# A decoder layer of three head groups on one core: both keys groups computed as a pair with tokens stationary, then turned

## The reference

```python
h = rmsnorm(x, norm_g)
q_a, k_a, v_a, g_a, u_p, g_p, q_m, g_m = split(h @ w_in)   # 1024 x4, 512 x4 columns
mem_k, mem_v = split(rmsnorm(mem, mem_norm_g) @ w_mem_kv)   # 256 memory tokens, 512 + 512
y_a = causal_attention(q_a, k_a, v_a) * silu(g_a)           # 8 heads x 128, one block of 256 keys
y_p = window_means(u_p) @ w_pool * pool_scale * silu(g_p)
y_m = memory_attention(q_m, mem_k, mem_v) * silu(g_m)       # 4 heads x 128
out = rmsnorm(x + concat(y_a, y_p, y_m) @ w_out, final_norm_g)
```

## Time and profile before

| | us |
|---|---|
| median of three executions | 429.81 (429.79 to 430.31) |
| the profiled execution | 429.81 |
| its span | 428.0 |
| TensorE busy | 419.6 |
| VectorE busy | 304.0 |
| ScalarE busy | 241.5 |
| GpSimd busy | 39.6 |

### The profile page before, as it was taken

The page is one execution under the profiler, slowest core; times in us unless marked ns, Lnnn a source line. Parts: engine busy times, 40 slices in busy tenths (PEclk is TensorE's granted clock), DMA queues, the critical chain, the costliest instruction groups (busy, mean ns, idle before and its releaser), DMA issues.

```text
span 428.0 us, 5922 instructions
## 1 busy us (share of the span) xinstructions
PE 419.6 (98%) x2244; PEld 361.7 (85%) x2244; DVE 304.0 (71%) x331; ACT 241.5 (56%) x325; POOL 39.6 (9%) x64
## 2 busy tenths in 40 slices
PE   9999999999999999999999999999999999999993
PEld 8888888888888888888888888888899888888882
DVE  5876865266786699857466878877667488897853
ACT  6764784284263766464465446555565566765611
POOL 1000000000050000000000232302000211000160
PEclk9999999999999999999999999999999999999998
DMA  8999969989979628645337256565646999468023
GB/s 277 415 413 420 410 201 371 131 270 361 157 185 270 249 100 306 222 159 196 100 106 239 98 172 213 158 196 155 239 149 208 252 415 279 174 241 297 3 84 112
DMA packets 28251, 96.34 MB, mean 225 GB/s; under 512 B 3776, under 2 KB 4288, under 8 KB 27328
## 3 DMA queue, kind: packets, MB, share of 16 engines
q1 hardware_dynamic: 24624, 83.26, 57.7%
q0 software_dynamic: 1152, 4.19, 5.4%
q10 hardware_dynamic: 2448, 8.52, 5.1%
HBM read 93.87 MB, written 2.10 MB: 224 GB/s over the span
## 4 chain that ended last, share of the span: by engine, by line
PE 95%; issue 2%; DVE 1%; POOL 0%; POOLq 0%; DVEq 0%
PE ps L622 36%; PE ps L625 18%; PE ps L640 4%; PE ps L638 4%; PE ps L639 4%; PE ps L681 3%; PE ps L679 3%; PE ps L680 3%; PE ps L662 3%; PE ps L664 3%; PE ps L663 3%; PE ps L603 3%; PE ps L610 1%; PE ps L759 1%; PE ps L714 1%
## 5 line engine op out<-in xcount | busy, mean ns | idle before, releaser
L1097 DVE TENSOR_TENSOR w_lo<-w_raw,w_hi 128x1024 fp32r<-128x1024 f32 x133 | 165.7, 1262 | 74.0 <-ACT w_hi L862 73.6
L622 PE MATMUL ps<-xT,w_hi 128*128 128x512 f32 x640 | 202.0, 397 | 0.0
L862 ACT ACTIVATE w_hi<-w_raw 128x1024 fp32r<-128x1024 f32 x133 | 138.0, 1055 | 84.0 <-PE ps L625 60.7
L625 PEld LDWEIGHTS ps<-xT,w_lo 128*128 128x128 f32 x640 | 120.2, 188 | 28.4
L625 PE MATMUL ps<-xT,w_lo 128*128 128x256 f32 x640 | 125.8, 278 | 0.0
L622 PEld LDWEIGHTS ps<-xT,w_hi 128*128 128x128 f32 x640 | 97.8, 189 | 0.4
L974 ACT ACTIVATE part_b<-ps 128x1024 f32<-128x1024 f32 x11 | 11.3, 1025 | 17.7 <-PE ps L625 17.7
L638 PE MATMUL ps<-w_hi,yT 128*128 128x512 f32 x46 | 17.9, 389 | 0.0
L639 PE MATMUL ps<-w_lo,yT 128*128 128x512 f32 x46 | 17.9, 389 | 0.0
L640 PE MATMUL ps<-w_hi,yT 128*128 128x512 f32 x46 | 17.9, 389 | 0.0
L862 ACT ACTIVATE w_hi<-x_f 128x1024 fp32r<-128x1024 f32 x8 | 8.5, 1060 | 10.5 <-PE ps L681 5.1
(11 more groups left out here) (208 smaller groups left out, 620.5 us busy)
## 6 DMA issues: line engine op xcount, KB each, us to landing
w_raw<-in_w_in SPq DMA_DIRECT2D x94, 512.0 KB, 4.5
w_raw<-in_w_out SPq DMA_DIRECT2D x30, 512.0 KB, 5.2
w_raw<-in_w_mem_kv SPq DMA_DIRECT2D x13, 512.0 KB, 12.4
x_t_raw<-in_x_t SPq DMA_DIRECT2D x8, 256.0 KB, 13.0
rows<-in_x ACTq DMA_DIRECT2D x2, 1024.0 KB, 9.9
rows<-in_mem ACTq DMA_DIRECT2D x2, 1024.0 KB, 12.6
x_f<-in_w_in SPq DMA_DIRECT2D x4, 512.0 KB, 6.7
x_f<-in_w_in POOLq DMA_DIRECT2D x4, 512.0 KB, 11.5
```

Of the source, the lines that this page charges most:

```text
L622: pe.matmul(ps[:, bank0(g) + f, :], hi[:, t, f * P:(f + 1) * P], moving[:, kt], start=(kt == 0), stop=(kt == KT - 1), skip_group_check=True)
L625: m = pe.matmul(ps[:, bank0(g) + f, 0:S], lo[:, t, f * P:(f + 1) * P], moving[:, kt, 0], start=False, stop=(kt == KT - 1), skip_group_chec ...
L862: act.activation(halves_of(n)[0], whole_of(n), ACT.Copy).then_inc(hi_done, 1)
L1097: dve.tensor_tensor(lo, whole_of(n), hi.bitcast(F32), ALU.subtract).then_inc(lo_done, 1)
```

## The change

K0 and K1 become a pair too, units 32 to 53, and the values' pair follows at units 54 to 75. Both use the same sums of activations. The keys then end with tokens on the rows, in `k_tok`; sixteen transposes on TensorE after the tenth unit of the values' pair (`turn_keys`) turn them, and ACT copies them to `kT`. In return for the features-on-rows form, 1/rms is multiplied in when the keys leave the accumulators, and no row of 1/rms is needed for them.

With it move: the sums of activations from K0's units to Q0's (`X_SUM_STEPS`); the loads and adding transfers of the pair's sums from K0's stretch to between Q1's loads; new ones for the values' pair into `v_f4` and again `x_f567`; the memory's rows into buffers of their own, at the same unit 20; the reading back of `rstd_rows` from unit 24 to 28 and from 36 to 46 (the writes stay at 22 and 34); and POOL's scaling of the memory's keys behind all eight adding transfers. The line numbers of the changed kernel are other ones.

```diff
-PAIRS = ((V0, V1), (OUT1, OUT2))
...
+PAIRS = ((K0, K1), (V0, V1), (OUT1, OUT2))
+KP, VP, OP = range(len(PAIRS))
+PAIR_UNITS = tuple(pair_units(*p) for p in PAIRS)
+PAIR_LOADS = tuple(pair_loads(*p) for p in PAIRS)
...
+K_PAIR = K0 * PPG
+V_PAIR = K_PAIR + IN_PAIR
+V_END = V_PAIR + IN_PAIR
...
-X_SUM_STEPS = {K0 * PPG + 2: 0, K0 * PPG + 3: 1, K0 * PPG + 4: 2, K0 * PPG + 5: 3}
...
+X_SUM_STEPS = {Q0 * PPG + 2: 0, Q0 * PPG + 3: 1, Q0 * PPG + 4: 2, Q0 * PPG + 5: 3}
...
-X_MEAN, MEM_MEAN = 20, 32
-SPREAD_WRITE, SPREAD_READ = {22: 0, 34: 1}, {24: 0, 36: 1}
+X_MEAN, MEM_MEAN = 20, 31
+SPREAD_WRITE, SPREAD_READ = {22: 0, 34: 1}, {28: 0, 46: 1}
+K_TWO, K_TURNED, K_COPIED = V_PAIR + 6, V_PAIR + 9, V_PAIR + 11
...
-            with sp.Fori(0, K1 - Q0) as g:
-                for a in range(PPG):
-                    sp.wait_ge(lo_done, g * PPG + (PPG + a + 1))
-                    sp.dma_start(w_raw[:, a], in_dram[bass.ds(g, 1), a].rearrange("g p t c -> p (g t) c")
-                                 ).then_inc(landed[a], 16)
+                load(p, dram, g - OUT0 if q == OP else IN_COLUMN[g], a)
+
+            def first_of_sums(q, f, dst, dram, column):
+
+                for i in range(BLOCKS):
+                    sp.dma_start(dst[:, i], dram[column, 2 * i]).then_inc((f4_landed, f5_landed)[f][q][i], 16)
+
+            for a in range(PPG):
+                sp.wait_ge(lo_done, MV * PPG + a + 1)
+                load(Q0 * PPG + a, in_dram, IN_COLUMN[Q0], a)
             for a in range(PPG):
                 if a == 1:
                     sp.wait_ge(x_lo, PPG)
-                    for i in range(BLOCKS):
-                        sp.dma_start(x_f4[:, i], in_dram[V1 - Q0, 2 * i]).then_inc(f4_landed[0][i], 16)
+                    first_of_sums(KP, 0, x_f4, in_dram, IN_COLUMN[K1])
                 if a == 5:
-                    for i in range(BLOCKS):
-                        sp.dma_start(x_f567[:, i, 0], in_dram[V0 - Q0, 2 * i]).then_inc(f5_landed[0][i], 16)
-                sp.wait_ge(lo_done, K0 * PPG + a + 1)
-                load(K1 * PPG + a, in_dram, K1 - Q0, a)
-            for r, (g, a) in enumerate(V_LOADS):
+                    first_of_sums(KP, 1, x_f567[:, :, 0], in_dram, IN_COLUMN[K0])
+                sp.wait_ge(lo_done, Q0 * PPG + a + 1)
+                load(Q1 * PPG + a, in_dram, IN_COLUMN[Q1], a)
+            for r, (g, a) in enumerate(PAIR_LOADS[KP]):
...
-                pair_load(0, V_PAIR + r, in_dram, Q0, g, a)
+                    slot_free(KP, *PAIR_LOADS[KP][r - RAW])
+                if r == RAW:
+                    sp.wait_ge(squared, 8)
+                    first_of_sums(VP, 0, v_f4, in_dram, IN_COLUMN[V1])
+                pair_load(KP, FIRST_PIECE[KP] + r, in_dram, g, a)
+            for r, (g, a) in enumerate(PAIR_LOADS[VP]):
+                if r < RAW:
...
+                if r == 4:
+                    sp.wait_ge(lo_done, unit_in(KP, M4, BLOCKS - 1) + 1)
+                    first_of_sums(VP, 1, x_f567[:, :, 0], in_dram, IN_COLUMN[V0])
+                pair_load(VP, FIRST_PIECE[VP] + r, in_dram, g, a)
...
-            for i in range(2):
+            def rstd_of(i):
+
...
+            rstd_of(0)
+            add_f4(KP, x_f4, in_dram, IN_COLUMN[K0])
+            add_f5(KP, x_f567, in_dram, IN_COLUMN[K0])
+            rstd_of(1)
+            add_f4(VP, v_f4, in_dram, IN_COLUMN[V0])
+            add_f5(VP, x_f567, in_dram, IN_COLUMN[V0])
+            pool.wait_ge(evacuated, V1 + 1)
             pool.wait_ge(rstd_spread[1], 16)
             pool.tensor_tensor(mkT[:, :, :], mkT[:, :, :], mem_rstd[:, :, :].to_broadcast([P, NF, M]),
                                ALU.mult).then_inc(mk_scaled, 1)
...
+            def turn_keys():
+
+                pe.wait_ge(evacuated, K1 + 1)
+                for f in range(2 * NF):
+                    for h in range(TH):
+                        c = (f % 2) * S + h * P
+                        m = pe.transpose(ps[:, bank0(K0) + f // 2, c:c + P], k_tok[:, h, f * HD:(f + 1) * HD], ident[:, :])
+                m.then_inc(k_turned, 1)
...
+                if n == K_PAIR:
+                    pe.wait_ge(evacuated, Q0 + 1)
                 if n == V_PAIR:
-                    pe.wait_ge(evacuated, K0 + 1)
-                if V_PAIR <= n < V_END:
+                    pe.wait_ge(evacuated, Q1 + 1)
+                if in_pair(n):
                     unit_of_pair(n)
+                    if n == K_TURNED:
+                        turn_keys()
                     continue
...
+                if a == 0 and g == U:
+                    pe.wait_ge(kT_ready, 2)
...
+            def spread(n):
+
+                if n in SPREAD_WRITE:
+                    i = SPREAD_WRITE[n]
+                    act.wait_ge(rstd_ready, i + 1)
+                    for h in range(TH):
+                        act.dma_start(rstd_rows[i, h].rearrange("(p a) -> p a", a=1), rstd_in[:, i, h:h + 1]
+                                      ).then_inc(rstd_written[i], 16)
+                if n in SPREAD_READ:
+                    i = SPREAD_READ[n]
+                    act.wait_ge(rstd_written[i], 16 * TH)
+                    act.dma_start((x_rstd, mem_rstd)[i][:, 0, :], rstd_rows[i].rearrange("(a h) p -> a (h p)", a=1)
+                                  .partition_broadcast(P)).then_inc(rstd_spread[i], 16)
+
...
+                    if n == K_COPIED:
+                        act.wait_ge(k_turned, 1)
+                        act.wait_ge(f67_done, sums_done(VP, F6, BLOCKS - 1))
+                        for j in range(2):
+                            act.activation(kT[:, NF * j:NF * (j + 1), :].rearrange("p (b f) s -> p b (f s)", b=2),
+                                           ps[:, bank0(K0) + 2 * j:bank0(K0) + 2 * j + 2, :], ACT.Copy).then_inc(kT_ready, 1)
...
-                        evacuate(K1)
+                    if n == K_PAIR + 12:
+                        evacuate(Q1)
+                    if n == K_PAIR + 16:
+                        dve.wait_ge(rstd_ready, 1)
+                        first_of_pair(*of_keys)
+                    if n == K_TWO:
+                        second_of_pair(*of_keys)
                     if n == V_PAIR + 16:
-                        values_one()
```

More of the change, by code:

```diff
@@ L152, in build @@
         qT = sb("qT", [P, 2 * NF, S], F32, early)
+        stage = ExitStack()
+        mem_rows_a = sb("mem_rows_a", [P, D], F32, stage)
+        stage.close()
+        stage = ExitStack()
+        v_f4 = sb("v_f4", [P, BLOCKS, TPP, COLS], F32, stage)
+        stage.close()
         kT = sb("kT", [P, 2 * NF, S], F32, early)
@@ L377, in whole_of @@
             g, i = unit(n)
-            sums4, sums567 = ((x_f4, x_f567), (f4, f567))[pair_of(n)]
+            sums4, sums567 = ((x_f4, x_f567), (v_f4, x_f567), (f4, f567))[pair_of(n)]
             return sums4[:, i] if g == N5 else sums567[:, i, {M4: 0, M1: F6, N7: F7}[g]]
@@ L539, in _ @@
                                ALU.mult).then_inc(mk_scaled, 1)
-            for k in range(BLOCKS):
-                pool.wait_ge(f4_landed[0][k], 16)
-                pool.dma_start(x_f4[:, k], in_dram[V0 - Q0, 2 * k], accum_op=ALU.add).then_inc(f4_summed[0][k], 16)
-            for k in range(BLOCKS):
-                pool.wait_ge(f5_landed[0][k], 16)
-                pool.dma_start(x_f567[:, k, 0], in_dram[V0 - Q0, 2 * k + 1], accum_op=ALU.add).then_inc(f5_summed[0][k], 16)
             def block_sums(i):
@@ L670, in pair_piece @@
                 g, a = unit(n)
-                rows = (xT, yT)[pair_of(n)]
+                rows = yT if pair_of(n) == OP else xT
                 for t in range(TPP):
@@ L1101, in weight_sum @@
                 p = piece_of(unit_in(q, M6 if f == F6 else M3, i))
-                sums4, sums567 = ((x_f4, x_f567), (f4, f567))[q]
+                sums4, sums567 = ((x_f4, x_f567), (v_f4, x_f567), (f4, f567))[q]
                 dve.wait_ge(landed[p % RAW], 16 * (p // RAW + 1))
@@ L1136, in split_sums, with first_of_pair @@
                                   ALU.subtract).then_inc(s_split, 1)
[L1138 removed]
+            def first_of_pair(qp, dst, scales):
                 first = slice(0, COLS)
[L1141 to L1143 removed]
+                one, two = PAIRS[qp]
+                dve.wait_ge(snapped, snaps_done(qp, SNAPS[M4, 1]))
+                settle(dve.tensor_tensor(dst[:, 1, first], dst[:, 1, first],
```

191 lines of the change are left out of this document (95 added, 96 removed).

## The result

The changed kernel takes 442.4 us (median of five executions, 441.6 to 443.6), the kernel before 429.8 on the same chip: a ratio of 1.0293, 95% interval 1.0274 to 1.0312. Slower, as forecast, but 5.4 us more than the 437 predicted and 1.4 above the range. The profiled execution took 443.6 us, with a span of 441.8.

The account below looks back on a forecast made before the run. TensorE's work was taken to bound the kernel. 428.0 - 1.7 (TensorE's work) + 8.3 (late Q1 piece) + 1.0 (ACT's lost lead) = 435.6 us of span, plus 1.8 outside it: 437 us, range 428 to 441.

Parts of the forecast that it names:

- What bounds the kernel, and the wait that takes over: Whole kernel: TensorE's work bounds it, 419.6 of 428.0 us; then TensorE idles before Q1's last units for late pieces, 8.3 us.
- TensorE's sum: Keys' pair and transposes on TensorE: -3.8 us for pairing, +1.75 for transposes, +0.3 for a wait, in all -1.7 us.
- the wait: Before the transposes in the values' pair: TensorE waits for DVE to take K1's half out, 0.3 us, bounds 0 and 1.4.
- ACT's chain: Start of the keys' pair: ACT, without lead, still has two squares, a copy and high parts to do; 1 us more.
- the first rival: Q1's loads: adds at the plain price, write delays nobody, last piece lands at 86.5, no wait; 428.1 us, chance 0.18.
- The bill of the moved transfers: DMA queue before Q1's last piece: transfers sum to 35.1 us, landing at 97.5, 8.3 us after the needed 89.2.
- The write of `rstd_rows`: Among Q1's loads, issued at 69.55: DMA engines then move next to nothing; lost time 3.5 to 5.3 us, taken as 4.5.
- Two adding transfers for `x_f567`: Around Q1's last two pieces: these start as those move and share the DMA engines with them; up to 5.8 us.
- The second write at 0 to 4.5: Keys' pair, unit 34: the write finds an emptier queue and costs 0, at most another 4.5 us.
- half of it: Q1's loads: write's stop or second adds fall outside, landing at 91.8 to 93; 428.5 to 433 us, chance 0.22.
- the third, the fallen clock: Behind a wait for a late piece: four units at half clock, up to 4 x 2.8 us more; 441 to 446, chance 0.05.
- The rule weighed against it: Q1's loads: 2.0 us per transfer plus bytes at 436 GB/s, adds unpriced; queue ends at 84 us, no wait, 428.1 us.

Follow-up runs that it names:

- everything out of the way: The change with three Q1 pieces before the wait for `xT`, `x_f567` loads after Q1's last, memory's rows at unit 16, writes at 64 and 76; 428.3 us.
- the write moved: The changed kernel with x's 1/rms written after unit 44 instead of 22 and read back after 50 instead of 28; 432.5 us.
- `x_f567` last: The changed kernel with the two loads for `x_f567` issued behind Q1's last piece instead of ahead of its last three; 447.2 us.
- plain adds: The changed kernel with the keys' pair's four adding transfers as plain loads, additions left out, write left in place; 436.1 us.

## Why the prediction missed, and what of it was right

**What bounds the kernel, and the wait that takes over: right.** Eleven loads from 59.5 on, TensorE idle in front of Q1's last units behind a load of `w_raw`, no wait above 0.2 us in the keys' pair: as written. The low GB/s came later and lasted longer, from 81 to 90 instead of 77 to 83.

**TensorE's sum: right.** From the start of the keys' pair to U are 84.8 us (193.17 - 108.41). The prediction's terms give twice 40.81, 1.75 for the transposes, 0.3 for the wait and 1.0 for ACT's chain: 84.7. The transposes took 1.97 and did not wait, and the first four half units took 6.42 (108.41 to 114.83) instead of 5.44, which is the 1.0 for ACT's chain. Without waits the change was worth what the sum on TensorE said: 428.3 was measured with everything out of the way, against 428.1 worked out for the first rival.

**The bill of the moved transfers: the step that failed.** Q1's last piece landed at 103.06 instead of 97.5. That is 5.6 us, and the time is off by 5.4. The path was right, its size was not: two terms of the bill were mis-sized, in opposite directions:
- "The write of `rstd_rows`": 4.5 us, with 3.5 to 5.3 as bounds. It cost 13.2. The bounds were lost time read where one piece at a time or a few stood beside the write. Beside a queue of plain loads the same write cost 7.6, beside adds 13.2, where its stop came twice. So bounds from the emptier stretch did not hold in the crowded one, and the sum had no term for what write and adds cost together, 5.6 us.
- "Two adding transfers for `x_f567`": 5.8 us. With the write gone, the bill up to Q1's last piece is 89.82 - 62.45 = 27.4 us, where the prediction has 35.1 - 4.5 = 30.6; so the terms without the write were 3.2 too large. I put that to this one, by the landings and not by a run of its own: with the write moved these two adds landed at 90.4 and 95.0, behind Q1's last piece at 89.8. The price of an add, 2.9 us, may have been too high as well: the four cost 4.2 us more than plain loads, where the prediction's prices give 6.6.

The rest of the bill stands: plain loads, memory's rows and plain transfers in place of the adds are 23.1 us (85.57 - 62.45). The prediction's prices give 21.5 with two such transfers and 24.0 with four.

**The second write at 0 to 4.5: right in time, partly by luck.** In the change nothing waited for it. But the queue was not so empty that the write made no hole; by stretch, in the changed kernel:

```profile
120.00:125.00 5.00, 5.00 (x24) 4.14 (x23) 4.95 (x5) 3.28 (x5) 0.00 (x0) 1.00 1.36 79
```

TensorE works all of these five us, since it had pieces enough. In the kernel with `x_f567` last it had not, and the wait was 7.4 us.

**The rivals.** The burst was not absorbed, and the time lies above what "half of it" gave. The time lies where the third, the fallen clock, had put it (441 to 446), but not for its reason: the clock fell (0.50 from 90 to 100), unit 29 ran slowly, and units 30 and 31 waited for their pieces anyway. Where the pieces were there, with plain adds, the same fall cost 2.2 us.

**The rule weighed against it.** From the fit that the Trainium skill gives (DMA: Bandwidth & Descriptors, Anatomy of one DMA), for a transfer that GpSimd issues, the prediction estimated the queue's end at 84 us. Without adds and write it was 85.6, so the trace is near it for plain transfers, most of them SP's; with adds and write it is 19 us off. The Trainium skill (DMA: Bandwidth & Descriptors, Specifications) says that below 512 bytes the DMA engine reads, modifies and writes. That alone does not tell eight bytes from four; here 128 elements of eight cost 1.4 to 2.3 us and of four 6.6 to 7.4, so it does not explain the hole.
